# Expert matmuls of a two-layer diffusion step: tokens held in 32-column groups, four quarters of the weights streamed beside each other, 4 KB weight rows, quarter-row scatters, and one activation table set for logarithm and exponential

## The chip, the core and the metric

The kernel runs on one core of one Trainium2 chip. The metric is the device time of one execution in microseconds (us), the median of several runs. All data are 32-bit floats. An fp32 matmul shows in the profile as two records, each with its own weight load.

## The reference

One inference step of a two-layer trunk over 640 tokens of width 1024: 128 context tokens and 512 latent tokens. Each layer is a norm with adaptive modulation, a token mixer (layer 0 an mLSTM, layer 1 a gated DeltaNet, both in two directions), a residual add, a second norm with modulation, and an expert-choice mixture of 16 SwiGLU experts:

```python
aff = softmax((x @ w_router).astype(float32), -1)
gsel, idx = lax.top_k(swapaxes(aff, 1, 2), cap)      # cap = 2 T / 16
xs = x[bidx, idx]
hdn = silu(einsum('becd,edf->becf', xs, w_gate)) * einsum('becd,edf->becf', xs, w_up)
out = einsum('becf,efd->becd', hdn, w_down) * gsel[..., None]
return zeros_like(x).at[bidx, idx].add(out)
```

Each expert takes 64 latent and 16 context tokens (80 in all) and has three weight matrices of 1024 x 1024, 12.58 MB together. The two layers have 32 experts, so 402.7 MB of expert weights are read once each. A final norm closes the trunk.

## The kernel before

The order of work is written out by hand for each engine, with semaphores between them. Per layer: modulation (twelve 2 MB blocks of `w_ada`, two rows of conditioning held in 32 columns, four quarters of the output streamed into PSUM partitions 0, 32, 64, 96: L766), norm and transposes, projections (L809, L810, L819), the scan, `mixer_tail` (`gate_tile`, output projection L1145, second norm, transposes L780, router logits L1151), then `experts`.

`experts` begins on VectorE with softmax and a top-k of ten rounds. TensorE transposes values and indices (L1190, L1191). A gather on GpSimd brings the 80 rows of an expert from `xn_d` into `xs`; `turn` (L1199) transposes them; `tokens` on VectorE (L1742, L1746) applies the modulation and writes `xsT`. `keep_clock` (L1229) is filler work for TensorE before the first expert.

For each expert `hidden` on TensorE (L1210) holds a 128 x 128 block of gate or up weights and streams the 80 tokens past it: 4 slots of 2 MB, 4 column blocks, 8 row blocks, so 128 matmuls or 256 records. ScalarE takes a tanh of the gate part (L689), VectorE makes SwiGLU of it in two operations (L1754, L1757) and writes `hdT`. `down` (L1221) holds 80 columns of `hdT` and streams 512 columns of the down weights: 16 matmuls, 32 records. ScalarE scales the result by the token's gate (L695), and GpSimd scatters 80 rows of 4 KB with accumulation into `moe_d` (L391). The order on TensorE is `hidden(e)`, `turn(e + 1)`, `down(e)`.

The six weight slots are single buffers. Each is loaded again for the next expert once its matmuls are done: slots 1, 3, 5 from the SyncE queue (L336), slots 0, 2, 4 from the ScalarE queue (L683). A slot is half of the columns of a matrix, so a row in HBM is 2 KB. VectorE copies the indices of an expert into `idc` and its gates into `gsc` (L1733, L1734) once the scatter of two experts before has landed.

After the last expert SyncE waits for the last scatter, reads `moe_d` back (L346) and VectorE adds it to `x` (L1784, L1785).

`inverse_root` on ScalarE (L425 Ln, L426 Exp) serves every norm; ScalarE loads a table before each of the two.

Of the kernel before, what the change touches and what calls it, by code (L numbers as in the profile page):

```python
# [24 lines left out]
P = 128  # L25
# [8 lines left out]
CAP = CAPS + CAPP  # L34
HC = 512
# [13 lines left out]
           gathered=256, gexp=32, gmm=1, h_chain=32, hidden=32, idx=16, logits=1, moe_used=96, o_ready=32,  # L49
           omm=10, scattered=256, selt=1, sel=2, sme=1, sm=1, st_new=4, topk=1, x_moe=5, x_new=10, xs_a=64,  # L50
# [3 lines left out]
def backbone(nc, a):  # L54
# [18 lines left out]
    with ctx:  # L73
# [49 lines left out]
        vals = sb("vals", [EX, CAP])  # L123
        idx = sb("idx", [EX, CAP], U32)
        idf = sb("idf", [EX, CAP])
        gsel = sb("gsel", [P, EX])
# [5 lines left out]
        moe_d = nc.dram_tensor("moe_d", [TOK, D], F32, kind="Internal").ap()  # L132
# [3 lines left out]
        osb = [og[:, (2 + q) * D:(3 + q) * D] for q in range(2)]  # L136
        hdT = og[:, 4 * D:4 * D + KT * CAP].rearrange("p (k c) -> p k c", k=KT)
        xsT = [wk[:, q * 640:(q + 1) * 640].rearrange("p (k c) -> p k c", k=KT) for q in range(2)]
        eb = [wk[:, 1280 + q * 320:1600 + q * 320] for q in range(2)]
# [24 lines left out]

        def w_expert(L, e, j):
# [90 lines left out]
        def _(sp):  # L256
# [22 lines left out]
            for L in range(2):  # L279
                for n in range(NADA + NIN):  # L280
                    j = mix_slot(n)
                    if n < 3:
                        if L:
                            sp.wait_ge(S("moe_used"), 6 * (EX - 1) + j + 1)
                    else:
                        sp.wait_ge(*unit_used(L, n - 3))
# [44 lines left out]
                def expert_loads(e, first):  # L331

                    for j in range(6) if first else (1, 3, 5):
                        if not first:
                            sp.wait_ge(S("moe_used"), L * PER["moe_used"] + e * 6 + (j - 5))
                        sp.dma_start(slot[j], w_expert(L, e, j)).then_inc(land[j], 16)  # L336
# [3 lines left out]
                expert_loads(0, True)  # L340
                with sp.Fori(1, EX) as e:
                    expert_loads(e, False)

                sp.wait_ge(S("scattered"), L * PER["scattered"] + 16 * EX)
# [11 lines left out]
        @block.gpsimd  # L356
        def _(pool):
            pool.memset(epst[:, :], EPS).then_inc(S("epst"), 1)

            for L in range(2):  # L360
# [10 lines left out]
                def hold(before):  # L371


                    if not (isinstance(before, int) and before == 0):
                        pool.wait_ge(S("held"), before)
                    pool.tensor_tensor(tick[:, 0:1], epst[0:1, :], epst[0:1, :], ALU.mult).then_inc(S("held"), 1)

                def gather(e, q, first):
                    pool.wait_ge(S("idx"), L * PER["idx"] + e + 1)
                    if not first:  # L380
                        pool.wait_ge(S("xs_turned"), L * PER["xs_turned"] + e - 1)
                    hold(2 * EX * L + e if first else e * 2 + (2 * EX * L - 1))
                    pool.indirect_dma_start(xs[q][0:CAP, :], None, xn_d,
                                            bass.IndirectOffsetOnAxis(ap=idc[q][0:CAP, :], axis=0)).then_inc(S("gathered"), 16)

                def scatter(e, q, first):
                    pool.wait_ge(S("o_ready"), L * PER["o_ready"] + e * 2 + 2)
                    if not first:
                        pool.wait_ge(S("scattered"), L * PER["scattered"] + e * 16)
                    hold(2 * EX * L + (2 * EX - 1) if e is EX - 1 else e * 2 + (2 * EX * L + 2))  # L390
                    pool.indirect_dma_start(moe_d, bass.IndirectOffsetOnAxis(ap=idc[q][0:CAP, :], axis=0),  # L391
                                            osb[q][0:CAP, :], None, compute_op=ALU.add).then_inc(S("scattered"), 16)

                pool.wait_ge(S("xn_out"), 16 * NT * (L + 1))
                pool.wait_ge(S("zero_out"), 16 * NT * (L + 1))
                gather(0, 0, True)
                gather(1, 1, True)
                scatter(0, 0, True)
                gather(2, 0, False)
                scatter(1, 1, False)  # L400
                with pool.Fori(1, EX // 2 - 1) as i:
                    for q in range(2):
                        gather(i * 2 + (q + 1), 1 - q, False)
                        scatter(i * 2 + q, q, False)
                gather(EX - 1, 1, False)
                scatter(EX - 2, 0, False)
                scatter(EX - 1, 1, False)
                pool.wait_ge(S("scattered"), L * PER["scattered"] + 16 * EX)
# [3 lines left out]
        def _(act):  # L412
# [14 lines left out]

            act.wait_ge(S("vec"), 1)
# [224 lines left out]
            def mixer_tail(L):  # L653

                i = 2 * L + 1
                gate_tile(L, 0)
# [18 lines left out]
            def experts(L):  # L675
# [3 lines left out]
                def expert(e, q, first, last=False):  # L679

                    def load(j):
                        if not last:
                            act.dma_start(slot[j], w_expert(L, e + 1, j)).then_inc(land[j], 16)  # L683

                    for hf in range(2):
                        act.wait_ge(S("moe_used"), L * PER["moe_used"] + e * 6 + (2 * hf + 1))
                        if first != 0:
                            act.wait_ge(S("hidden"), L * PER["hidden"] + e * 2 + (hf - 1))
                        A(eb[hf], PS[:, 2 * hf, 0:320], ACT.Tanh, scale=0.5).then_inc(S("gexp"), 1)  # L689
                        load(2 * hf)  # L690
                    for hf in range(2):
                        act.wait_ge(S("moe_used"), L * PER["moe_used"] + e * 6 + (5 + hf))
                        if hf == 0 and first is None:
                            act.wait_ge(S("scattered"), L * PER["scattered"] + (e - 1) * 16)
                        A(osb[q][0:CAP, hf * HC:(hf + 1) * HC], PS[0:CAP, 4 + hf, :], ACT.Copy,  # L695
                          scale=gsc[q][0:CAP, :]).then_inc(S("o_ready"), 1)
                        if hf == 0:
                            load(4)

                expert(0, 0, 0)  # L700
                expert(1, 1, 1)
                with act.Fori(1, EX // 2 - 1) as i:
                    for q in range(2):
                        expert(i * 2 + q, q, None)
                expert(EX - 2, 0, None)
                expert(EX - 1, 1, None, last=True)
# [8 lines left out]
            for L in range(2):  # L715
                norm(2 * L)
# [13 lines left out]
                experts(L)  # L730
            norm(4)
# [3 lines left out]
        def _(pe):  # L735
# [447 lines left out]
            def experts(L):  # L1183
# [6 lines left out]
                tr(PS[0:CAP, 3, 0:EX], vals[:, :], ident[0:EX, 0:EX])  # L1190
                tr(PS[0:CAP, 3, EX:2 * EX], idf[:, :], ident[0:EX, 0:EX]).then_inc(S("selt"), 1)  # L1191
                pe.wait_ge(S("sel"), L * PER["sel"] + 2)

                def turn(e, q, first):
                    pe.wait_ge(S("gathered"), L * PER["gathered"] + e * 16 + 16)
                    if not first:
                        pe.wait_ge(S("xs_in"), L * PER["xs_in"] + e)
                    for kt in range(KT):
                        ins = tr(PS[:, 6 + kt // 4, (kt % 4) * CAP:(kt % 4 + 1) * CAP], xs[q][0:CAP, kt * P:(kt + 1) * P], ident[0:CAP, 0:CAP])  # L1199
                    ins.then_inc(S("xs_turned"), 1)  # L1200

                def hidden(e, q, first):
                    pe.wait_ge(S("xs_in"), L * PER["xs_in"] + e + 1)
                    for j in range(4):
                        pe.wait_ge(land[j], e * 16 + (16 * moe_base(L, j) + 16))
                        if not first:
# [650 lines left out]
```

## Time and profile before

| | us |
|---|---|
| median of 3 runs | 3200.09 (3190.57 to 3201.3) |
| profiled execution, its own time | 3194.56 |
| its span, first to last instruction | 3192.6 |
| TensorE busy | 2937.7 (92%) |
| VectorE, ScalarE, GpSimd busy | 963.5, 567.1, 95.9 |
| DMA | 545.49 MB, mean 171 GB/s |

TensorE's records overlap and their ends are modelled, so a busy TensorE need not be one at its peak. A record of 512 columns is shown as 592 ns at full clock while the next one starts after some 430. The granted clock has two levels, 1.2 and 2.4 GHz; 1.00 in a row is 2.4. The experts of layer 0 run from 741.5 to 1431.1 us of the span, those of layer 1 from 2458.7 to 3148.4.

### The profile page before, as it was taken

The numbers are of one execution on the slowest core, as the hardware profiler recorded it, in microseconds if no ns is written. First come the engines' busy times: TensorE is split into PE (matmuls) and PEld (weight loads), VectorE is DVE, ScalarE is ACT, GpSimd is POOL, SyncE is SP. The second block draws the span as 40 slices with busy tenths as digits, with TensorE's granted clock in tenths as the row PEclk, the third lists the DMA queues.
The fourth block names the chain that finished last, engine by engine and source line by source line (L and its number), as shares of the span: only waits on it lengthen the run. The fifth ranks groups of instructions, "written<-read, shape, count | busy, mean of one in ns | idle before, by whom it ended". The sixth has DMA issues, their size and how long they took to land.

```text
span 3192.6 us, 43116 instructions
## 1 busy us (share of the span) xinstructions
PE 2937.7 (92%) x18357; PEld 2213.0 (69%) x18357; DVE 963.5 (30%) x2409; ACT 567.1 (18%) x1279; POOL 95.9 (3%) x145
## 2 busy tenths in 40 slices
PE   4999999788999999994999989999896999999994
PEld 1565489556778877771665479999845778887773
DVE  1100156542011100002577346677544011100002
ACT  2100111340000000002474112222251000000002
POOL 0000000000000000000000000000000000000000
PEclk8999998888999999997899989999997999999997
DMA  8312000247999999949211000000026899998892
GB/s 355 115 53 73 0 1 1 66 157 255 309 308 305 308 310 305 308 158 385 71 53 53 14 1 1 1 1 1 7 80 239 302 307 307 313 309 303 305 309 82
DMA packets 257932, 545.49 MB, mean 171 GB/s; under 512 B 15233, under 2 KB 23817, under 8 KB 251657
## 3 DMA queue, kind: packets, MB, share of 16 engines
q1 hardware_dynamic: 156617, 328.64, 29.1%
q10 hardware_dynamic: 93600, 188.75, 16.9%
q0 software_dynamic: 7584, 26.22, 3.3%
q8 instruction: 99, 1.62, 0.2%
q14 instruction: 32, 0.26, 0.0%
HBM read 517.89 MB, written 25.70 MB: 170 GB/s over the span
## 4 chain that ended last, share of the span: by engine, by line
PE 85%; DVE 6%; DMA 5%; ACT 3%; issue 1%; SPq 1%; DVEq 0%; POOL 0%; ACTq 0%
PE ps L1210 29%; PE ps L1221 14%; PE ps L809 9%; PE ps L819 6%; PE ps L1145 4%; DMA slots<-in_w_ada_dram 3%; PE ps L1107 3%; PE ps L810 2%; PE ps L1089 2%; PE ps L886 2%; PE ps L1121 1%; PE ps L766 1%; PE ps L797 1%; PE ps L956 1%; PE ps L972 1%; PE ps L968 1%
## 5 line engine op out<-in xcount | busy, mean ns | idle before, releaser
L1210 PEld LDWEIGHTS ps<-wk,slots 128*128 128x128 f32 x6144 | 691.1, 192 | 16.5 <-issue 16.0
L1210 PE MATMUL ps<-wk,slots 128*128 128x80 f32 x6144 | 689.9, 275 | 0.0
L1221 PE MATMUL ps<-qkv,og 128*80 128x512 f32 x1024 | 446.7, 594 | 2.4 <-DVE og L1757 1.3
L1221 PEld LDWEIGHTS ps<-qkv,og 128*80 128x80 f32 x1024 | 151.0, 150 | 275.4 <-issue 268.0
L809 PE MATMUL ps<-hT,slots 128*128 128x512 f32 x640 | 333.3, 603 | 3.3 <-ACT hT L457 3.3
L1210 PE MATMUL ps<-wk,qkv 128*128 128x80 f32 x2048 | 233.9, 275 | 0.0
L810 PEld LDWEIGHTS ps<-hT,slots 128*128 128x128 f32 x640 | 123.2, 193 | 156.1 <-issue 156.1
L1210 PEld LDWEIGHTS ps<-wk,qkv 128*128 128x128 f32 x2048 | 231.3, 192 | 0.0
L819 PE MATMUL ps<-slots,hT 128*128 128x512 f32 x480 | 208.9, 595 | 0.0
L1733 DVE COPY idc<-idT 80x1 uint32 (+1 forms) x32 | 4.8, 149 | 615.1 <-DMA moe_d<-og,idc 615.0
L819 PEld LDWEIGHTS ps<-slots,hT 128*128 128x128 f32 x480 | 91.6, 191 | 111.6 <-issue 111.3
L695 ACT ACTIVATE og<-ps,gsc 80x512 f32<-80x512 f32 x64 | 43.7, 683 | 657.7 <-PE ps L1221 657.7
L689 ACT ACTIVATE wk<-ps 128x320 f32<-128x320 f32 x64 | 28.0, 437 | 717.7 <-PE ps L1210 717.7
L1145 PE MATMUL ps<-slots,qkv 128*128 128x512 f32 x320 | 140.7, 598 | 7.0 <-DMA slots<-in_w_out_dram 4.7
L766 PE MATMUL ps<-slots,cndP 128*32 128x512 f32 x384 | 68.5, 854 | 76.4 <-DMA slots<-in_w_ada_dram 51.9
L1757 DVE SCALAR_TENSOR_TENSOR og<-wk,ps 128x320 f32<-128x320 f32 x64 | 31.2, 487 | 323.9 <-PE ps L1210 323.9
L810 PE MATMUL ps<-hT,slots 128*128 128x128 f32 x640 | 124.1, 276 | 0.0
L1754 DVE SCALAR_TENSOR_TENSOR wk<-wk,ps 128x320 f32<-128x320 f32 x64 | 31.1, 487 | 284.8 <-ACT wk L689 284.1
L1145 PEld LDWEIGHTS ps<-slots,qkv 128*128 128x128 f32 x320 | 60.6, 192 | 80.3 <-issue 75.3
L1495 DVE SCALAR_TENSOR_TENSOR wk<-wk,vecT 128x128 f32<-128x128 f32 x192 | 106.0, 552 | 6.8
L809 PEld LDWEIGHTS ps<-hT,slots 128*128 128x128 f32 x640 | 99.8, 195 | 4.2 <-ACT hT L457 3.7
L1107 PE MATMUL ps<-wk,slots 128*128 128x64 f32 x800 | 100.2, 279 | 2.6 <-DVE wk L1627 2.6
(262 smaller groups left out, 3134.8 us busy)
## 6 DMA issues: line engine op xcount, KB each, us to landing
slots<-in_w_gate_dram ACTq DMA_DIRECT2D x60, 2048.0 KB, 10.1
qkv<-in_w_down_dram SPq DMA_DIRECT2D x34, 2048.0 KB, 9.8
slots<-in_w_up_dram SPq DMA_DIRECT2D x32, 2048.0 KB, 10.1
qkv<-in_w_up_dram SPq DMA_DIRECT2D x32, 2048.0 KB, 7.9
qkv<-in_w_down_dram ACTq DMA_DIRECT2D x30, 2048.0 KB, 7.8
slots<-in_w_ada_dram SPq DMA_DIRECT2D x24, 2048.0 KB, 12.8
slots<-in_w_in_dram SPq DMA_DIRECT2D x16, 2048.0 KB, 8.3
slots<-in_w_out_dram SPq DMA_DIRECT2D x4, 2048.0 KB, 16.4
```

What stands on the lines that cost most here:

```text
L695: A(osb[q][0:CAP, hf * HC:(hf + 1) * HC], PS[0:CAP, 4 + hf, :], ACT.Copy, scale=gsc[q][0:CAP, :]).then_inc(S("o_ready"), 1)
L766: ins = mm(PS[32 * j:32 * (j + 1), g % 2, :], cndP[:, kt, :], aslot[sl][:, kk, j * HC:(j + 1) * HC], start=(kt == 0), stop=(kt == KT - 1))
L809: mm(PS[:, b, :], w, hT[:, kt, P:TOK], start=(kt == 0), stop=(kt == KT - 1))
L810: ins = mm(PS[:, b + 1, 0:P], w, hT[:, kt, 0:P], start=(kt == 0), stop=(kt == KT - 1))
L819: ins = mm(PS[:, 2 * (i % n), :], hT[:, kt, t * P:(t + 1) * P], slot[sl][:, kt, :], start=(kt == 0), stop=(kt == KT - 1))
L886: mm(PS[:, bank, h * P:(h + 1) * P], src[:, h:h + 1].broadcast_to([P, P]), ident, start=(h == 0), stop=False, skip_group_check=True)
L1089: ins = mm(pack(four(PS[:, bx, :])[:, :, 0:64], l)[:, h], B["CM"][l % 2][:, h, :], cols1(B["D"][:, h, :], l, d), start=True, stop=True)
L1107: ins = mm(hb(2 * p + l % 2, h, 64), B["DT"][:, h, :], B["X"][:, h, :], start=True, stop=True)
L1145: ins = mm(PS[:, 6 + j, :], yT[:, kt, t * P:(t + 1) * P], slot[j][:, kt, :], start=(kt == 0), stop=(kt == KT - 1))
L1210: ins = mm(PS[:, j, fb * CAP:(fb + 1) * CAP], slot[j][:, kt, fb * P:(fb + 1) * P], xsT[q][:, kt, :], start=(kt == 0), stop=(kt == KT - 1))
L1221: ins = mm(PS[0:CAP, 4 + j, :], hdT[:, ft, :], slot[4 + j][:, ft, :], start=(ft == 0), stop=(ft == KT - 1))
L1495: ins = V.scalar_tensor_tensor(o_, s, w, o_, ALU.mult, ALU.add)
```

## The change

The 80 tokens are padded to 96 and cut into three groups of 32 (`NGRP`). For gate and up TensorE holds 32 tokens of one row block in each of its four 32-column groups and streams a different quarter of the weight columns past each (256 of gate and 256 of up, 512 in all), so that quarter q lands in partitions 32q to 32q + 31: `gate_up` is 2 halves x 3 groups x 4 row blocks x 4 quarters = 96 matmuls of 512 columns. The hidden values come out with tokens on partitions, so `turn_hidden` transposes them back in six 128 x 128 transposes and ScalarE evacuates them to `hdT`. `down` is 96 matmuls of 256 columns in the same form. The order on TensorE becomes first half of gate and up of e, `turn(e + 1)`, second half, `down(e - 1)`, `turn_hidden(e)`. All loops over experts are unrolled.

A weight block is now half of the rows of a matrix with all columns: 2 MB in rows of 4 KB, all from the SyncE queue. Gathers read their indices from `idT` directly and run up to four experts ahead. The result of an expert is scattered in three DMAs of 128 quarter rows of 1 KB; padded tokens go to 16 extra rows of `moe_d`. Their indices and gates, replicated over the four quarters, come from 24 small matmuls before the first expert.

On ScalarE `log_and_exp` loads the set that holds both functions at five places: the start, each `mixer_tail`, the start of layer 1 and before the final norm.

```diff
+NGRP = 3
+CAPG = 32 * NGRP
+PAD = CAPG - CAP
+HQ = D // 4
...
-        idc = [sb(f"idc{q}", [P, 1], U32) for q in range(2)]
-        gsc = [sb(f"gsc{q}", [P, 1]) for q in range(2)]
+        idQ = sb("idQ", [P, NGRP, EX], U32)
...
+        moe_d = nc.dram_tensor("moe_d", [TOK + PAD, D], F32, kind="Internal").ap()
+        moe_q = moe_d.rearrange("t (q c) -> (t q) c", q=4)
...
         def w_expert(L, e, j):
-            name, hf = (("w_gate", 0), ("w_up", 0), ("w_gate", 1), ("w_up", 1), ("w_down", 0), ("w_down", 1))[j]
-            return a[name][L].rearrange("e (k p) n -> e p k n", p=P)[e, :, :, hf * HC:(hf + 1) * HC]
+            name, hf = (("w_gate", 0), ("w_up", 0), ("w_down", 0), ("w_gate", 1), ("w_up", 1), ("w_down", 1))[j]
+            dst = wdn[hf] if name == "w_down" else wgu[hf][:, j % 3, :, :]
+            return dst, a[name][L].rearrange("e (k p) n -> e p k n", p=P)[e, :, 4 * hf:4 * hf + 4, :]
...
@@ block.sync
+                for e in range(EX):
+                    if e:
+                        sp.wait_ge(S("gu_half"), L * PER["gu_half"] + e)
+                    expert_load(e, 0)
+                    expert_load(e, 1)
+                    if e:
+                        sp.wait_ge(S("gu_done"), L * PER["gu_done"] + NGRP * e)
+                    expert_load(e, 3)
+                    expert_load(e, 4)
+                    if e:
+                        sp.wait_ge(S("dn_half"), L * PER["dn_half"] + e)
+                    expert_load(e, 2)
+                    if e:
+                        sp.wait_ge(S("dn_done"), L * PER["dn_done"] + NGRP * e)
+                    expert_load(e, 5)
...
@@ block.gpsimd
+                def gather(e):
+                    if e >= 2:
                         pool.wait_ge(S("xs_turned"), L * PER["xs_turned"] + e - 1)
+                    hold()
+                    pool.indirect_dma_start(xs[e % 2][0:CAP, :], None, xn_d,
+                                            bass.IndirectOffsetOnAxis(ap=idT[0:CAP, e:e + 1], axis=0)).then_inc(S(f"gathered{e % 2}"), 16)
+                def scatter(e):
+                    if e:
+                        pool.wait_ge(S("scattered"), L * PER["scattered"] + 16 * NGRP * e)
+                    for g in range(NGRP):
+                        pool.wait_ge(S("o_ready"), L * PER["o_ready"] + NGRP * e + g + 1)
+                        hold()
+                        pool.indirect_dma_start(moe_q, bass.IndirectOffsetOnAxis(ap=idQ[:, g, e:e + 1], axis=0),
+                                                osb[e % 2][:, g, :], None, compute_op=ALU.add).then_inc(S("scattered"), 16)
...
+                for e in range(4):
+                    gather(e)
+                for e in range(EX):
+                    if e + 4 < EX:
+                        gather(e + 4)
+                    scatter(e)
...
@@ block.scalar
+            def log_and_exp():
+                nc.scalar.preload_act_table_set("natural_log_exp_and_others")
...
             def mixer_tail(L):
+                log_and_exp()
                 gate_tile(L, 0)
...
+                def gate(e, g):
+                    act.wait_ge(S("gu_done"), L * PER["gu_done"] + NGRP * e + g + 1)
+                    if e:
+                        act.wait_ge(S("hid_tr"), L * PER["hid_tr"] + e)
+                    A(hid[:, g, :], PS[:, g, 0:HQ], ACT.Tanh, scale=0.5).then_inc(S("gexp"), 1)
+                def out(e, g):
+                    act.wait_ge(S("dn_done"), L * PER["dn_done"] + NGRP * e + g + 1)
...
+                    A(osb[e % 2][:, g, :], PS[:, 5 + g, 0:HQ], ACT.Copy, scale=gselT[:, g, e:e + 1]).then_inc(S("o_ready"), 1)
+                def turned_hidden(e):
+                    act.wait_ge(S("hid_tr"), L * PER["hid_tr"] + e + 1)
...
+                    A(hdT[:, 0:2, :, :, :].rearrange("p g b q c -> p (g b q c)"), PS[:, 3, :], ACT.Copy).then_inc(S("hid_ev"), 1)
+                    A(hdT[:, 2, :, :, :].rearrange("p b q c -> p (b q c)"), PS[:, 4, 0:HQ], ACT.Copy).then_inc(S("hid_ev"), 1)
...
@@ block.tensor
+                for k, src in enumerate((idf, vals)):
+                    for g in range(NGRP):
+                        i = 1 + NGRP * k + g
+                        for q in range(4):
+                            ins = mm(PS[32 * q:32 * (q + 1), 3, i * EX:(i + 1) * EX], src[:, 32 * g:32 * (g + 1)], ident[0:EX, 0:EX],
+                                     start=True, stop=True)
...
+                def gate_up(e, hf, g, kt):
+                    for q in range(4):
+                        ins = mm(PS[32 * q:32 * (q + 1), g, :].rearrange("p (a n) -> p a n", a=2), xsT[e % 2][:, 4 * hf + kt, 32 * g:32 * (g + 1)],
+                                 wgu[hf][:, :, kt, q * HQ:(q + 1) * HQ], start=(hf + kt == 0), stop=(hf == 1 and kt == 3))
+                    return ins
+                def down(e, hf, g, kt):
+                    qq, b = divmod(4 * hf + kt, 2)
+                    for q in range(4):
+                        ins = mm(PS[32 * q:32 * (q + 1), 5 + g, 0:HQ], hdT[:, g, b, qq, :],
+                                 wdn[hf][:, kt, q * HQ:(q + 1) * HQ], start=(hf + kt == 0), stop=(hf == 1 and kt == 3))
+                    return ins
...
+                def gate_up_all(e):
+                    pe.wait_ge(S("xs_in"), L * PER["xs_in"] + e + 1)
+                    weights(e, 0, 1)
+                    for kt in range(4):
+                        for g in range(NGRP):
+                            ins = gate_up(e, 0, g, kt)
+                    ins.then_inc(S("gu_half"), 1)
+                    if e + 1 < EX:
+                        turn(e + 1)
+                    weights(e, 3, 4)
+                    for g in range(NGRP):
+                        for kt in range(4):
+                            ins = gate_up(e, 1, g, kt)
+                        ins.then_inc(S("gu_done"), 1)
+                def down_all(e):
+                    pe.wait_ge(S("hid_ev"), L * PER["hid_ev"] + 2 * e + 2)
...
+                def turn_hidden(e):
+                    if e + 1 < EX:
+                        pe.wait_ge(S("xs_in"), L * PER["xs_in"] + e + 2)
+                    for g in range(NGRP):
+                        pe.wait_ge(S("hidden"), L * PER["hidden"] + NGRP * e + g + 1)
+                        for b in range(2):
+                            c = g % 2 * HQ + b * P
+                            ins = tr(PS[:, 3 + g // 2, c:c + P], hid[:, g, b * P:(b + 1) * P], ident)
+                    ins.then_inc(S("hid_tr"), 1)
...
+                for e in range(EX):
+                    gate_up_all(e)
+                    if e:
+                        down_all(e - 1)
+                    turn_hidden(e)
+                down_all(EX - 1)
...
@@ block.vector
+                def hidden(e, g):
...
+                    V.scalar_tensor_tensor(hid[:, g, :], hid[:, g, :], 1.0, PS[:, g, 0:HQ], ALU.add, ALU.mult).then_inc(k, 1)
...
+                    V.scalar_tensor_tensor(hid[:, g, :], hid[:, g, :], 0.5, PS[:, g, HQ:2 * HQ], ALU.mult, ALU.mult).then_inc(S("hidden"), 1)
```

## Rows read from the trace of the kernel before

**Rows 1.** The page's chain that ended last, share of the span by line.

```profile
PE ps L1210 29%; PE ps L1221 14%; PE ps L809 9%; PE ps L819 6%; PE ps L1145 4%; DMA slots<-in_w_ada_dram 3%; PE ps L1107 3%; PE ps L810 2%; PE ps L1089 2%; PE ps L886 2%; PE ps L1121 1%; PE ps L766 1%; PE ps L797 1%; PE ps L956 1%; PE ps L972 1%; PE ps L968 1%
```

**Rows 2.** The chain in order of time: start us, us, what.

```profile
741.54 28.56 PE ps L1210 x256
770.73 13.96 PE ps L1221 x32
...
1417.19 13.97 PE ps L1221 x32
```

**Rows 3.** Windows: stretch, PE, PEld, DVE, ACT, POOL busy, PEclk, DMA share, GB/s.

```profile
13.00:18.00 5.00, 0.89 (x3) 0.46 (x3) 1.26 (x5) 0.21 (x1) 0.00 (x0) 1.00 1.00 410
22.00:32.00 10.00, 4.81 (x28) 1.10 (x32) 2.77 (x10) 9.84 (x16) 0.00 (x0) 1.00 1.01 421
720.00:730.00 10.00, 0.00 (x0) 0.00 (x0) 9.49 (x25) 0.00 (x0) 0.00 (x0) 0.50 1.05 387
800.00:1400.00 600.00, 599.54 (x4117) 472.81 (x4116) 56.65 (x165) 31.39 (x56) 37.30 (x54) 1.00 0.90 306
```

**Rows 4.** Timeline of TensorE: start us, us, engine, line, operation, count [idle before].

```profile
30.83 1.92 PE L766 MATMUL ps<-slots,cndP 128*32 128x512 f32 x16 [1.24 <-DMA slots<-in_w_ada_dram]
31.29 0.13 PEld L766 LDWEIGHTS ps<-slots,cndP 128*32 128x32 f32 x4 [0.30 <-issue]
31.72 0.13 PEld L766 LDWEIGHTS ps<-slots,cndP 128*32 128x32 f32 x4 [0.30 <-issue]
297.40 7.03 PE L819 MATMUL ps<-slots,hT 128*128 128x512 f32 x16
```

**Rows 5.** Groups by form, 800 to 1400 us: busy us, mean ns | idle before.

```profile
L695 ACT ACTIVATE og<-ps,gsc 80x512 f32<-80x512 f32 x28 | 19.1, 684 | 288.1 <-PE ps L1221 288.1
L1754 DVE SCALAR_TENSOR_TENSOR wk<-wk,ps 128x320 f32<-128x320 f32 x28 | 13.7, 488 | 120.0 <-ACT wk L689 119.3 <-issue 0.3
L689 ACT ACTIVATE wk<-ps 128x320 f32<-128x320 f32 x28 | 12.2, 437 | 283.8 <-PE ps L1210 283.8
L1199 PE MATMUL ps<-c,og 80*128 80x80 f32 x112 | 10.1, 232 | 0.0
```

**Rows 6.** DMA, 13 to 18 us: what moved; then the page's software queue.

```profile
DMA packets 537, 2.05 MB, mean 410 GB/s; under 512 B 20, under 2 KB 44, under 8 KB 533
q0 software_dynamic: 7584, 26.22, 3.3%
```

**Rows 7.** Timeline before the first expert of layer 0.

```profile
697.00 10.26 PE L1151 MATMUL ps<-wrt,hT 128*128 128x16 f32 x48
730.93 0.24 PE L1190 MATMUL ps<-c,vals 16*80 16x16 f32 x1 [20.75 <-DVE idf L1723]
731.02 0.22 PE L1191 MATMUL ps<-c,idf 16*80 16x16 f32 x1
```

**Rows 8.** Timeline after the last expert of layer 0.

```profile
1432.30 1.44 POOL L391 DMA_INDIRECT moe_d<-og,idc  x1 [0.16 <-issue]
1437.49 2.55 SPq L346 DMA_DIRECT2D og<-moe_d  x5
```

**Rows 9.** Groups of ScalarE over the whole span: its table loads.

```profile
L425 ACT ACT_TABLE_LOAD x51 | 65.4, 1283 | 0.9
L426 ACT ACT_TABLE_LOAD x51 | 65.4, 1283 | 0.9
```

**Rows 10.** Timeline of the end of layer 0's mixer and of the final norm.

```profile
672.37 13.97 PE L1145 MATMUL ps<-slots,qkv 128*128 128x512 f32 x32 [1.14 <-DVE x L1680]
695.26 1.94 PE L780 MATMUL ps<-c,og 128*128 128x128 f32 x8 [3.70 <-DVE hT L1326]
3176.60 0.15 DVE L1305 TENSOR_SCALAR ss<-ss 128x1 f32<-128x1 f32 x1
3178.57 0.15 DVE L1305 TENSOR_SCALAR ss<-ss 128x1 f32<-128x1 f32 x1
3188.26 1.28 DVE L1317 SCALAR_TENSOR_TENSOR og<-x,ss,wk 128x1024 f32<-128x1024 f32 x1
```

More of the change, by code:

```diff
@@ L330, in _, with expert_load @@
                     sp.dma_start(xn_d[t * P:(t + 1) * P, :], o[:, t, :]).then_inc(S("xn_out"), 16)
[L331 to L336, printed above, removed]
+                def expert_load(e, j):
+                    dst, src = w_expert(L, e, j)
+                    sp.dma_start(dst, src).then_inc(land[j], 16)
                 sp.wait_ge(*unit_used(L, MIX - 1))
                 sp.wait_ge(S("x_new"), L * PER["x_new"] + 10)
[L340 to L344, printed above, removed]
+                for e in range(EX):
[13 more added lines that the diff above has]
+                    expert_load(e, 5)
+                sp.wait_ge(S("scattered"), L * PER["scattered"] + 16 * NGRP * EX)
                 for t in range(NT):
@@ L358, in _ @@
             pool.memset(epst[:, :], EPS).then_inc(S("epst"), 1)
+            held = [0]
             for L in range(2):
@@ L369, in _, with hold @@
                     pool.dma_start(moe_d[t * P:(t + 1) * P, :], zero).then_inc(S("zero_out"), 16)
-                def hold(before):
-                    if not (isinstance(before, int) and before == 0):
-                        pool.wait_ge(S("held"), before)
+                pool.dma_start(moe_d[TOK:TOK + PAD, :], zero[0:PAD, :]).then_inc(S("zero_out"), 16)
+                for q in range(2):
+                    pool.memset(xsT[q][:, :, CAP:CAPG], 0.0).then_inc(S("xs_pad"), 1)
+                def hold():
+                    if held[0]:
+                        pool.wait_ge(S("held"), held[0])
@@ L386, in scatter @@
[L386 to L392, printed above, removed]
@@ L394, in _ @@
-                pool.wait_ge(S("xn_out"), 16 * NT * (L + 1))
[L395 to L404, printed above, removed]
@@ L677, in experts @@
                 A(aff[:, :, :], aff[:, :, :], ACT.Exp).then_inc(S("sme"), 1)
[L679 to L698, printed above, removed]
@@ L708, in modulation @@
+                for e in range(EX + 1):
+                    if e < EX:
+                        for g in range(NGRP):
+                            gate(e, g)
+                    if e:
+                        for g in range(NGRP):
+                            out(e - 1, g)
+                    if e < EX:
+                        turned_hidden(e)
             def modulation(L):
@@ L1189, in experts @@
                 pe.wait_ge(S("topk"), L * PER["topk"] + 1)
[L1190 to L1197, printed above, removed]
+                pe.wait_ge(S("pads"), 5 + PAD)
@@ L1214, in down @@
-                def down(e, q, first):
-                    pe.wait_ge(S("hidden"), L * PER["hidden"] + e * 2 + 2)
-                    for j in range(2):
-                        pe.wait_ge(land[4 + j], e * 16 + (16 * moe_base(L, 4 + j) + 16))
-                        if not first:
-                            pe.wait_ge(S("o_ready"), L * PER["o_ready"] + e * 2 + (j - 1))
-                        for ft in range(KT):
-                            ins = mm(PS[0:CAP, 4 + j, :], hdT[:, ft, :], slot[4 + j][:, ft, :],
-                                     start=(ft == 0), stop=(ft == KT - 1))
-                        ins.then_inc(S("moe_used"), 1)
+                def gate_up(e, hf, g, kt):
[3 more added lines that the diff above has]
+                    return ins
@@ new lines, in down, with weights @@
+                def down(e, hf, g, kt):
[4 more added lines that the diff above has]
+                    return ins
+                def weights(e, *slots):
+                    for j in slots:
+                        pe.wait_ge(land[j], 16 * (moe_base(L, j) + e + 1))
@@ L1727, in experts @@
[L1727 to L1736 removed]
+                V.tensor_copy(idT[0:CAP, :], PS[0:CAP, 3, 0:EX]).then_inc(S("sel"), 1)
@@ L1779, in experts @@
+                tokens(0)
+                for e in range(EX):
+                    if e + 1 < EX:
+                        tokens(e + 1)
+                    for g in range(NGRP):
+                        hidden(e, g)
                 dve.wait_ge(S("g2b"), L * PER["g2b"] + 4)
```

170 lines of the change are left out of this document (72 added, 98 removed).

## The prediction

> **What bounds the kernel now.** The page's chain comes first: TensorE's lines carry it, L1210 with 29% and L1221 with 14%, both of the experts [rows 1]. The chain in order of time then gives the cycle. From 741.54 us on, 256 records of L1210 take 28.56 us and 32 of L1221 take 13.96; the sixteenth expert ends at 1417.19 + 13.97 = 1431.16. That is 689.6 us per layer, 43.1 per expert [rows 2], of which the 8 transposes of `turn` are some 0.6. In the window of 600 us TensorE is busy for 599.54 at full clock while the DMA share is 0.90 at 306 GB/s [rows 3], so nothing else ends last. What the change is worth is read from two rates. Why L1210 is slow is in the quotient: 28.56 / 256 = 0.112 us for a record that streams 80 columns, whereas L1221 needs 13.96 / 32 = 0.436 for 512. Per column that is 1.40 ns against 0.85; L1210's records are paced by their 128-column weight loads and not by the stream.
>
> **TensorE after the change.** The modulation already has the form that the experts get: 32 columns held, four quarters streamed. Its 16 records of 512 columns took 1.92 us at full clock, where 16 ordinary ones took 7.03, and its weight loads come in fours at 31.29 and 31.72, so four records start every 0.43 us [rows 4]. The four quarters do run beside each other, and 1.92 is four such steps plus the tail of the last. Per expert, with two records per matmul:
> - gate and up: 96 matmuls are 192 records, 48 steps of 0.43: 20.6 us (28.56 before);
> - down: 96 matmuls of 256 columns are 48 steps of half the columns, 0.215: 10.3 us (13.96 before);
> - `turn`: 8 transposes, 10.1 us for 112, so 0.7 [rows 5];
> - `turn_hidden`: 6 transposes at L1210's 0.112, so 0.7;
> - four changes between the whole array and its quarters. No row has such a change in a full stream. Below it is nothing; above, I take the tail that an isolated burst shows, 1.92 - 4 x 0.43 = 0.2 each. I take 0.7 together.
>
> The sum is 33.0 us. The down step is the weakest term, since no row streams 256 columns in quarters. Below, its columns bound it at 10.3; above, it could cost as much per step as gate and up do (0.43), 20.6. I take 10.3, because the quarter loads of a step are shown as only 0.13 us for four [rows 4], inside 0.215.
>
> **DMA after the change.** The present stage's weight rows are 2 KB, and with nothing else running they came at 387 GB/s; the start of the kernel, mostly `x` in rows of 4 KB, ran at 410, the 8 KB rows of `w_ada` at 421 [rows 3]. That the first is 4 KB shows in its packets, 2.05 MB in 537 [rows 6]. So 12.58 MB need 12.58 / 0.410 = 30.7 us. The gather adds 0.33 MB; the scatter moves 0.39, and an accumulation also reads what it adds to, so 0.39 to 0.79: 1.8 to 2.7 us at the same rate. Its 384 descriptors of 1 KB instead of 80 of 4 KB may cost more than their bytes; all software DMAs together took 3.3% of the span now, 105 us or at most 3.3 per expert [rows 6], and double the scatter's part would add 1 to 2. DMA needs 32.5 to 33.4, middle 32.9.
>
> TensorE's 33.0 and DMA's 32.9 are level. A load and its use are set apart, though: a block is freed after 10, 21, 27 or 32 us of the cycle and wanted again 10 us or more later than it lands, so neither has to wait for the other's single step and the cycle is the larger of the two. I take 33.2. ScalarE's eight operations per expert are at most 8 x 0.68, and VectorE's six SwiGLU operations at most 6 x 0.49 beside the token operations [rows 5]; both lie beside `down(e - 1)`. SyncE waits for first half, second half, then down's halves, which is TensorE's own order, so no load stands behind a later one. On GpSimd `gather(e + 4)` stands ahead of `scatter(e)` and waits for a transpose in the next expert's first half; `scatter(e)` needs a later point anyway. ScalarE waits for the scatter of three experts before, which has a cycle to land.
>
> **The ends of a layer's experts.** The first expert has no `down` to cover its tanh and SwiGLU of the last group: 0.44 + 0.49 + 0.49 and handovers, 1.7 us [rows 5]. The last `down` waits for the evacuation of `hdT`, under 2 x 0.68, 1.3 us. One `turn` less is -0.7. A layer is 16 x 33.2 + 2.3 = 533.5 against 689.6: 156.1 saved, 312 for both.
>
> The 24 small matmuls before the first gather are 48 records on the path. The two transposes there start 0.09 us apart, at half clock, and a router record with a full weight load takes 10.26 / 48 = 0.21 [rows 7]: 4.3 by the one, 10.3 by the other, and near 1 if the quarters overlap as in the modulation. I take 2.8, less 0.3 for `idc` and `gsc`, which go: +2.5 per layer, +5. After the last expert one scatter took 1437.49 - 1432.30 = 5.2 us, with 1.44 of GpSimd [rows 8]. Three follow each other now at 1.7 us, the groups' pace, and three of GpSimd's may take up to 2 each with 128 rows: 0 to +2, taken as +1 per layer, +2.
>
> **Table set.** 102 table loads of 1.28 us stand before Ln and Exp [rows 9]; 70 of them are in norms and gate tiles and go, the 32 of layer 1's q and k stay. Most are covered: by DMA at the start, by the output projection in the mixer's tail, by modulation in layer 1. On the path are, per layer, TensorE's wait of 3.70 us before the last transpose, of which two loads are 2.6, and 1.14 before the last projection tile, which waits for VectorE behind ScalarE's norms [rows 10]: 7.4 for both. One load stands ahead of layer 1's first gate tile, 1.3. In the final norm ScalarE paces the five tiles; without its loads VectorE does, from 3176.60 in steps of 1.97, ending at 3186.5 where it ended at 3188.26 + 1.28 = 3189.5 [rows 10]: 3.1. Together 11.8. Should the set not be kept, this is nothing.
>
> **Sum.** -312 + 5 + 2 - 12 = -317, against the profiled execution's own 3194.6 (its span is 3192.6): 2878. The median of the runs shown is 5.5 higher, so I say 2880.
>
> **Two rules of the Trainium skill.** TensorE's rows show sixteen quarter records in 1.92 us against 7.03, 3.7 times, and 4.0 times in their steady steps of 0.43 [rows 4]. "TensorE: Matmul & The Clock Gate", section "Measured speedup vs the span model", gives 3.07 times for four row tiles and 2.38 for three column tiles. An estimate from 3.07 would be 20.6 + 10.3 = 30.9 x 4 / 3.07 = 40.3, with 2.1 for the rest 42.4, and a time of some 3170. The steady step speaks against it, the lack of a burst longer than 16 records for it.
>
> The windows of this trace move 410 and 421 GB/s into the core [rows 3]. "DMA: Bandwidth & Descriptors", section "Where 436 GB/s comes from", puts an HBM limit of about 358 per core where its neighbour also streams. Here one core runs, and the trace is above it. By 358 the cycle would be 13.7 / 0.358 = 38 us, some 3030 in all.
>
> **Rivals.**
> - The stream of weights ends last. Where 4 KB rows come no faster than 2 KB rows among the scatters, 13.7 MB at 387 GB/s are 35.4 us [rows 3]; with the dearer small descriptors 36.5. For: the two needs are level, and nobody has shown 4 KB rows beside scatters. Against: 410 and 421. Only fifteen cycles a layer feel it: 15 x 2 x 2.2 to 3.3 = +66 to +99, so 2945 to 2980. Chance 0.18.
> - The quarters do not keep 0.43 and 0.215 in a long stream. If each group of four steps costs 1.92 as in the burst, gate and up are 23.0, down (with the same 0.05 per step) 12.7, the cycle 37.8: +147, 3025. If down's step costs what gate and up's does, 20.6 + 20.6 + 2.1 = 43.3, no gain from the experts, about 3200. Chance 0.11 for a cycle of 35 to 42.5 from this cause, 0.03 for no difference.
> - Slower than before: TensorE's supply of instructions. The cycle has 768 loads and records where it had 576, most for quarter-size work. No long stretch of rows shows them closer than L1210's, 512 in 28.56 us, 0.056 each. At that pace every step of eight costs 0.446, gate and up 21.4, down 21.4, the cycle 44.9: 2 x (16 x 44.9 + 2.3 - 689.6) = +62, less 5 for the rest: 3252. It decides from a down step of about 0.42 on. Against: L1210's pace is explained by its wide loads. Chance 0.05.
> - The change does not do what it says for the tables: the loads stay, +12, 2892. That lies inside the forecast's own spread.
>
> **Chances.** The forecast (cycle 32.3 to 34.5 us, 2850 to 2920) has 0.63. Faster by over 0.5%: 0.63 + 0.18 + 0.11 = 0.92; within 0.5% (16 us, about what a measurement of this kernel can tell from no change) 0.03; slower 0.05. The range 2845 to 2980 takes in the rival of the weight stream and leaves out some 0.19: the slow quarters and what follows them.
>
> **What would show it.** Chain and windows of a layer's middle: a cycle of 33.2 us at full clock. Steps of TensorE: 10.3 us for a half of gate and up, 5.2 for a half of down; a longer down half alone means its small steps, all halves longer alike means the quarters. A wait of TensorE on DMA before gate and up, with the DMA share at 1.00, means the stream; GB/s then tells its rate. Table loads: some 37 at L425 and L426 and the preloads. The experts of a layer outside 515 to 590 us would make the prediction wrong.

## The result, and the profile after

| | us |
|---|---|
| before, median of 4 runs | 3200.12 (3190.57 to 3201.3) |
| after, median of 4 runs | 3518.36 (3514.34 to 3522.01) |
| after / before | 1.1001, 95% interval 1.0977 to 1.1026 |
| predicted | 2880 (2845 to 2980) |

The changed kernel is 10% slower; faster was forecast. The page's chain after, share of the span by line (L1237 is gate and up, L1245 is down), shows what is new against [rows 1]; the line numbers of these two matmuls are others in some of the kernels below:

```profile
PE ps L1237 20%; DMA slots<-in_w_up_dram 17%; PE ps L1245 9%; PE ps L834 8%; PE ps L844 6%; PE ps L1170 4%; DMA slots<-in_w_ada_dram 3%; PE ps L1132 3%; PE ps L835 2%; PE ps L1114 2%; PE ps L911 1%; PE ps L1146 1%; SPq L342 1%; PE ps L791 1%; PE ps L822 1%
```

A transfer carries 17% of the span. The chain in order of time, one cycle of layer 0, answers to [rows 2]:

```profile
819.13 12.69 PE ps L1237 x96
831.82 0.70 PE ps L1231 x8
832.52 10.44 PE ps L1237 x96
842.96 10.40 PE ps L1245 x192
...
853.79 0.59 SPq L342
854.42 20.19 DMA slots<-in_w_up_dram
```

The next cycle's matmuls start at 874.75. TensorE's work is as forecast, but for the first half, which takes 12.69 us here instead of 10.3, and then it stands for 20 us. From the second expert of layer 0 (765.16) to its last (1543.84) are 14 cycles of 55.6 us, where 33.2 were forecast; the 14 of layer 1 are 55.8 each. The windows, in the columns of [rows 3], say the same of the DMA engines:

```profile
800.00:1400.00 600.00, 371.32 (x4200) 148.64 (x4204) 48.28 (x131) 36.20 (x85) 64.05 (x83) 0.80 0.66 242
874.80:908.50 33.70, 33.70 (x393) 13.39 (x394) 4.44 (x12) 2.10 (x5) 3.29 (x6) 0.95 0.41 155
908.50:929.90 21.40, 0.76 (x8) 0.55 (x9) 0.00 (x0) 1.34 (x3) 2.84 (x3) 0.59 1.05 389
```

Over the stage their share is 0.66 and TensorE's clock 0.80. While TensorE works the share is 0.41, inside the wait it is 1.05. So DMA works in full only while TensorE stands, and is idle for more than half of the time in which TensorE works. The reason is in SyncE's timeline, laid beside TensorE's:

```profile
903.32 0.37 SPq L342 DMA_DIRECT2D slots<-in_w_down_dram  x1
908.50 0.37 SPq L342 DMA_DIRECT2D qkv<-in_w_down_dram  x1
908.91 1.61 SPq L342 DMA_DIRECT2D slots<-in_w_gate_dram  x1
910.57 0.67 SPq L342 DMA_DIRECT2D slots<-in_w_up_dram  x1
911.28 4.48 SPq L342 DMA_DIRECT2D qkv<-in_w_gate_dram  x1
```

```profile
903.08 5.36 PE L1245 MATMUL ps<-qkv,wk 128*32 128x256 f32 x96
908.37 0.87 PE L1290 MATMUL ps<-c,wk 128*128 128x128 f32 x6
929.89 11.93 PE L1237 MATMUL ps<-slots,wk 128*32 128x512 f32 x96 [20.64 <-DMA slots<-in_w_up_dram]
```

The loads of gate and up for the next expert go out at 908.91, straight after the down projection ends, although their buffers had been free since the middle and the end of gate and up, some 22 and 11 us earlier.

### The profile page after: what moved, and what is told of

Same layout as the page of the kernel before. It is cut to its first block, busy times and chain, and to the rows that moved or that the text cites. A ratio compares the mean times of both kernels' runs of the same rounds, so it can differ in the third digit from the quotient of the medians.

```text
span 3514.8 us, 49131 instructions
## 1 busy us (share of the span) xinstructions
PE 2684.7 (76%) x21715; PEld 1582.1 (45%) x21715; DVE 976.9 (28%) x2432; ACT 522.4 (15%) x1341; POOL 206.3 (6%) x279
## 4 chain that ended last, share of the span: by engine, by line
PE 69%; DMA 22%; DVE 6%; SPq 1%; ACT 1%; issue 1%; POOL 0%; DVEq 0%; ACTq 0%; POOLq 0%
PE ps L1237 20%; DMA slots<-in_w_up_dram 17%; PE ps L1245 9%; PE ps L834 8%; PE ps L844 6%; PE ps L1170 4%; DMA slots<-in_w_ada_dram 3%; PE ps L1132 3%; PE ps L835 2%; PE ps L1114 2%; PE ps L911 1%; PE ps L1146 1%; SPq L342 1%; PE ps L791 1%; PE ps L822 1%
## 5 line engine op out<-in xcount | busy, mean ns | idle before, releaser
L1237 PE MATMUL ps<-slots,wk 128*32 128x512 f32 x3072 | 398.8, 682 | 587.3 <-DMA slots<-in_w_up_dram 587.3
L1237 PEld LDWEIGHTS ps<-slots,wk 128*32 128x32 f32 x3072 | 114.6, 124 | 851.1 <-issue 851.1
L1237 PE MATMUL ps<-qkv,wk 128*32 128x512 f32 x3072 | 336.2, 593 | 0.0
L705 ACT ACTIVATE wk<-ps 128x256 f32<-128x256 f32 x96 | 36.9, 384 | 1356.9 <-PE ps L1237 1356.9
L1237 PEld LDWEIGHTS ps<-qkv,wk 128*32 128x32 f32 x3072 | 97.0, 110 | 214.2 <-issue 211.6
L1245 PE MATMUL ps<-qkv,wk 128*32 128x256 f32 x3072 | 175.1, 384 | 5.1 <-DMA qkv<-in_w_down_dram 5.1
L1245 PE MATMUL ps<-slots,wk 128*32 128x256 f32 x3072 | 171.7, 379 | 5.1 <-DMA slots<-in_w_down_dram 5.1
L413 POOL DMA_INDIRECT moe_d<-og,idQ x96 | 149.5, 1557 | 30.6 <-POOL tick L397 28.7
L397 POOL TENSOR_TENSOR tick<-epst 1x1 f32<-1x1 f32 x128 | 47.4, 370 | 1580.5 <-PE ps L1231 787.8
L1245 PEld LDWEIGHTS ps<-slots,wk 128*32 128x32 f32 x3072 | 101.1, 110 | 82.5 <-issue 23.5
L1245 PEld LDWEIGHTS ps<-qkv,wk 128*32 128x32 f32 x3072 | 101.2, 111 | 73.4 <-DMA qkv<-in_w_down_dram 6.1
L1815 DVE SCALAR_TENSOR_TENSOR wk<-wk,ps 128x256 f32<-128x256 f32 x96 | 40.5, 422 | 319.7 <-ACT wk L705 319.7
```

Source lines behind the costliest of these rows:

```text
L413: pool.indirect_dma_start(moe_q, bass.IndirectOffsetOnAxis(ap=idQ[:, g, e:e + 1], axis=0), osb[e % 2][:, g, :], None, compute_op=ALU.add). ...
L1237: ins = mm(PS[32 * q:32 * (q + 1), g, :].rearrange("p (a n) -> p a n", a=2), xsT[e % 2][:, 4 * hf + kt, 32 * g:32 * (g + 1)], wgu[hf][:, : ...
L1245: ins = mm(PS[32 * q:32 * (q + 1), 5 + g, 0:HQ], hdT[:, g, b, qq, :], wdn[hf][:, kt, q * HQ:(q + 1) * HQ], start=(hf + kt == 0), stop=(hf ...
```

## The experiments

**The queue's order.** The theory: in the loop over e, SyncE issues gate and up of e, then waits for the down projection of e - 1, which TensorE runs after gate and up of e, and only then comes to gate and up of e + 1. The edit moves the down blocks behind the next expert's gate and up:

```diff
-                for e in range(EX):
...
+                for j in (0, 1, 3, 4, 2, 5):
+                    expert_load(0, j)
+                for e in range(1, EX + 1):
+                    if e < EX:
+                        sp.wait_ge(S("gu_half"), L * PER["gu_half"] + e)
+                        expert_load(e, 0)
+                        expert_load(e, 1)
+                        sp.wait_ge(S("gu_done"), L * PER["gu_done"] + NGRP * e)
+                        expert_load(e, 3)
+                        expert_load(e, 4)
+                    if e >= 2:
+                        sp.wait_ge(S("dn_half"), L * PER["dn_half"] + e - 1)
+                        expert_load(e - 1, 2)
+                        sp.wait_ge(S("dn_done"), L * PER["dn_done"] + NGRP * (e - 1))
+                        expert_load(e - 1, 5)
```

> The changed kernel with SyncE's loads in TensorE's order: blocks 0, 1, 3, 4 of expert e + 1 now stand ahead of blocks 2 and 5 of expert e, which wait for the down projection of e - 1... e's own predecessor. Theory, a queue behind a waiting instruction: in the changed kernel the gate and up loads of the next expert stood behind two waits on a down projection that runs last in the cycle, and TensorE stood 20 us for them. With the order mended the cycle falls from 54.9 to 33.2 us (TensorE 32.7, DMA 32.9) and the time to 2870 to 2900. Rival, the stream itself is slow: the changed kernel's DMA share of 0.66 over a cycle of 54.9 is 36 us of DMA work per expert; then the cycle is 36.3 and the time about 2970, with TensorE waiting some 3 us per expert.

Measured: 2906.87 us (2902.84 to 2913.45), 0.9093 of before (0.9077 to 0.911), the fastest of the kernels here that do the whole work. It is 7 us above the 2870 to 2900 of the theory and far below the rival's 2970. Its windows and TensorE's timeline:

```profile
850.00:1150.00 300.00, 286.33 (x3502) 137.17 (x3498) 37.17 (x100) 30.67 (x71) 53.98 (x70) 1.00 1.04 386
```

```profile
968.18 10.51 PE L1237 MATMUL ps<-slots,wk 128*32 128x512 f32 x96 [1.64 <-DMA slots<-in_w_up_dram]
980.45 10.51 PE L1237 MATMUL ps<-qkv,wk 128*32 128x512 f32 x96 [1.06 <-DMA qkv<-in_w_up_dram]
990.75 5.39 PE L1245 MATMUL ps<-slots,wk 128*32 128x256 f32 x96
995.93 5.39 PE L1245 MATMUL ps<-qkv,wk 128*32 128x256 f32 x96
1002.49 10.51 PE L1237 MATMUL ps<-slots,wk 128*32 128x512 f32 x96 [0.37 <-DMA slots<-in_w_up_dram]
```

The 20 us are gone, the clock is whole, and the DMA share is 1.04. Nine cycles, counted at the start of the second half of gate and up from 910.72 to 1221.97, are 34.6 us each. The order alone is worth 3518 - 2907 = 611 us. The cycle lies between the two expectations, 33.2 and 36.3: TensorE still waits 0.2 to 1.6 us twice per expert.

**Half of the wait.** Gate and up are put between the two down blocks:

```diff
+                    if e >= 2:
+                        sp.wait_ge(S("dn_half"), L * PER["dn_half"] + e - 1)
+                        expert_load(e - 1, 2)
...
+                        expert_load(e, 4)
+                    if e >= 2:
+                        sp.wait_ge(S("dn_done"), L * PER["dn_done"] + NGRP * (e - 1))
+                        expert_load(e - 1, 5)
```

> As the mended order, but gate and up of the next expert stand behind the first block of down (free after half of the down projection) and ahead of the second. Theory of the queue: they are held until half of the down projection is done, and 6.3 MB (one block of down, two of gate and up) then take 15.4 us at 410 GB/s plus 2; TensorE covers 5.9 of it, waits some 11.5, starts cold for 1.7: a cycle of 46, about 3270 us. Rival, the order only moves a wait that the stream makes: no more than the mended order, under 3000.

Measured, one run: 3348.56 us. TensorE's wait:

```profile
965.35 13.27 PE L1238 MATMUL ps<-slots,wk 128*32 128x512 f32 x96 [15.41 <-DMA slots<-in_w_up_dram]
```

The wait shrinks from 20.6 to 15.4 us, by the 5.2 us by which the release is earlier. So the wait follows the place of the load in the queue, with everything else of the change as it was. The cycle is 50.6 us (1015.93 for the next start) where I said 46, and the time 79 us above my 3270, because my number for the wait, 11.5, was too small: from 943.9 to the landing at 965.3 the engines moved 354 GB/s x 21.4 us = 7.6 MB, where I had counted 6.3. The scatters' 0.4 MB and parts of the blocks issued next, some 0.9 MB, were served in the same time.

**Another queue.** The down blocks are loaded from ScalarE's queue, behind the evacuation of e - 1:

```diff
                         for g in range(NGRP):
                             out(e - 1, g)
+                        if e < EX:
+                            for j in (2, 5):
+                                dst, src = w_expert(L, e, j)
+                                act.dma_start(dst, src).then_inc(land[j], 16)
```

> The changed kernel, but the two down blocks of expert e are loaded from the ScalarE queue once the results of e - 1 are evacuated, and SyncE's queue keeps only gate and up. No load order is copied from TensorE's. Theory, head of a queue: what cost the 20 us was that gate and up stood behind waits for the down projection, so taking those waits to another queue does as well as mending the order: a cycle of 34 to 35 us, 2900 to 2920. Rival: it was the mended kernel's finer release (the first down block after half of the down projection) that gave the gain; here both down blocks are released 5 us later, and the cycle would be 38 or more, over 3000.

Measured: 2932.88 us (2926.34 to 2934.08), 0.9178 of before (0.9163 to 0.9193). It loses 26 us to the mended order and lies 13 above the 2920 that I gave it at most, but it is far from the rival's 3000: what matters is that gate and up don't stand behind the down projection, whichever way. Its first down block is issued 5 us later, and between 850 and 1225 us TensorE waits five times, 1.4 to 4.9 us each, for the second half of gate and up. Behind a longer one of these waits that half is slow, at a lower clock:

```profile
882.92 13.32 PE L1235 MATMUL ps<-qkv,wk 128*32 128x512 f32 x96 [3.01 <-DMA qkv<-in_w_up_dram]
```

**TensorE alone.** Weights are loaded for the first expert of each layer only:

```diff
-                        pe.wait_ge(land[j], 16 * (moe_base(L, j) + e + 1))
+                        pe.wait_ge(land[j], 16 * (moe_base(L, j) + 1))
```

> The changed kernel with weights loaded for the first expert of each layer alone; all experts use them, so the expert part of the result is that of other weights. It leaves TensorE's own cycle. Theory: 32.7 to 33.0 us (48 steps of 0.43, 48 of 0.215, 0.7 and 0.7 for transposes, changes between whole array and quarters under 0.2 each), about 2870 us. Rival, long streams of quarters pay for the changes or for instruction supply: a cycle above 34.5.

Measured, one run: 2852.1 us. Window and timeline:

```profile
800.00:1200.00 400.00, 400.00 (x4848) 164.52 (x4844) 53.24 (x144) 41.36 (x96) 73.15 (x95) 1.00 0.15 23
```

```profile
962.38 10.51 PE L1224 MATMUL ps<-slots,wk 128*32 128x512 f32 x96
972.82 0.77 PE L1218 MATMUL ps<-c,og 80*128 80x80 f32 x8
973.52 10.51 PE L1224 MATMUL ps<-qkv,wk 128*32 128x512 f32 x96
983.84 5.36 PE L1232 MATMUL ps<-slots,wk 128*32 128x256 f32 x96
989.02 5.36 PE L1232 MATMUL ps<-qkv,wk 128*32 128x256 f32 x96
994.32 0.88 PE L1277 MATMUL ps<-c,wk 128*128 128x128 f32 x6
995.12 10.51 PE L1224 MATMUL ps<-slots,wk 128*32 128x512 f32 x96
```

The cycle is 995.12 - 962.38 = 32.74 us. A half of gate and up is 24 steps of 0.43 (10.44 and 10.32 to the next start), a half of down 24 of 0.216 (5.18 and 5.30). The half that is followed by whole-array transposes is 0.12 us longer each time, so little is lost between whole array and quarters. Both rivals about TensorE fall here.

**DMA alone, with three loads.** TensorE leaves out two of four row blocks in each half of gate, up and down (`kt in (0, 3)`), which was to leave it some 17 us of work; it was busy for 22 per cycle, at a granted clock of 0.80. The second kernel also has no scatters; the third has the scatters and reads each block in 2 KB rows:

```diff
-            return dst, a[name][L].rearrange("e (k p) n -> e p k n", p=P)[e, :, 4 * hf:4 * hf + 4, :]
+            return (dst.rearrange("p k (h n) -> p (k h) n", h=2),
+                    a[name][L].rearrange("e (k p) n -> e p k n", p=P)[e, :, :, hf * HC:(hf + 1) * HC])
```

> The kernel with the mended order, leaving out half of the row blocks of every expert matmul (two of four in each half), so that TensorE needs some 17 us per expert; all loads, gathers and scatters stay. Theory, the mended kernel is bound by DMA (share 1.04 at 387 GB/s): its cycle stays at 34 to 34.5 us and the time at 2895 to 2915. Rival, its 34.4 come from TensorE's short waits and starts, and DMA alone needs the predicted 32.9: a cycle near 33.

> As the kernel with half of the row blocks, and it also leaves out the scatters. Theory, the scatters' 1 KB rows with accumulation are what the prediction sized too small: weights and gathers alone come at 405 to 410 GB/s, 12.9 MB in 31.7 us, so the scatters cost 2.7 of 34.4. Rival, rows of 4 KB from the expert matrices come no faster than 387 GB/s: 33.3 us, the scatters cost 1.

> As the kernel with half of the row blocks, but each 2 MB block is read in rows of 2 KB (the same bytes and destinations' size, the weights themselves land in other places). Theory, longer rows matter: the cycle rises by the ratio of the shown rates, 410 / 387, to about 36.3. Rival, row length between 2 and 4 KB is nothing: the same cycle as with 4 KB.

Measured, one run each: 2862.41, 2790.96 and 2905.33 us. The same window of the three, in that order:

```profile
850.00:1150.00 300.00, 192.01 (x1800) 75.03 (x1800) 39.94 (x108) 28.74 (x67) 50.20 (x66) 0.80 1.04 389
```

```profile
850.00:1150.00 300.00, 200.20 (x1886) 80.49 (x1890) 39.93 (x108) 30.98 (x72) 9.76 (x18) 0.83 1.03 401
```

```profile
850.00:1150.00 300.00, 178.02 (x1668) 70.13 (x1672) 35.50 (x96) 27.58 (x64) 50.91 (x67) 0.79 1.06 371
```

From landing to landing the cycles are 34.4, 32.4 and 36.2 us (seven, eight and seven of them). With half the matmuls the cycle of the mended kernel, 34.6, hardly moves: it is bound by DMA, as expected. Its time of 2862 is below my 2895 to 2915, because the first and last experts, where the mended kernel goes at TensorE's pace, are shorter with half the matmuls. Scatters cost 2.0 us of the 34.4, and rows of 4 KB instead of 2 KB save 1.8. My price for the scatters, 2.7, and the rival's, 1, both miss; without them the stream runs at 401 GB/s and not at the 410 of [rows 3]. Each of these three is one run of one kernel.

**The cold start after the wait.** In the changed kernel the first half of gate and up takes 11.8 to 13.5 us instead of 10.5, at a clock that fell during the wait. Fillers stand in the wait:

```diff
                     turn_hidden(e)
+                    if e + 1 < EX:
+                        for _ in range(20):
+                            mm(PS[:, 0, :], ident, hT[:, 0, 0:HC], start=True, stop=True)
```

> The changed kernel with 20 filler matmuls (17 us of identity times 512 columns into a free PSUM bank) after each expert's hidden transposes, while TensorE would stand for the loads. Theory: the part of the 20 us wait that the queue makes is untouched, but the first half of gate and up no longer starts at 1.2 GHz: it takes 10.5 instead of 12.0 to 13.5 us, the cycle falls by about 2.2 and the time by 30 x 2.2 = 66, to about 3450. Rival: the time of the cold start is hidden by the loads' pace and comes back as wait: 3518.

> The changed kernel with 23 fillers instead of 20 after each expert's hidden transposes, 19.9 us, so that the gap of 3.8 us before the loads land, in which the clock fell again with 20 fillers, shrinks to about 1. Theory: the first half of gate and up then takes 10.5 instead of 12.0 to 13.4 us, the cycle falls by some 2.2 and the time by 30 x 2.2 to about 3450. Rival: the cold start is hidden, since the loads of the second half and of the next cycle set the pace: 3518, with a wait that grows by what the halves lose.

Measured, one run each: 3520.58 with 20 fillers and 3479.89 with 23, where I had expected about 3450 of both. With 20 a wait of 3.79 us was left, with a granted clock of 0.87 in it and of 0.78 in the half that followed, which still took 13.37. With 23 (the last two lines) the clock was 1.00 in both:

```profile
943.61 13.37 PE L1237 MATMUL ps<-slots,wk 128*32 128x512 f32 x96 [3.79 <-DMA slots<-in_w_up_dram]
...
976.04 19.91 PE L1310 MATMUL ps<-hT,c 128*128 128x512 f32 x46
996.66 10.51 PE L1237 MATMUL ps<-slots,wk 128*32 128x512 f32 x96 [0.71 <-DMA slots<-in_w_up_dram]
```

The half takes 10.51, and the fourteen cycles of layer 0, 783.48 to 1530.01, are 53.3 us, 2.3 less than 55.6. The whole kernel gains 38 and not 66 us: in front of each layer's second expert, where the real wait was only 1.7 and 2.7 us, the fillers add 17 to 18 and take more than half of the gain back. So the first run told only that 17 us of filler are too few; the second puts the cold start at 2.3 us a cycle, by estimate some 65 us of the result (28 x 2.3).

**The table set alone.** The five preloads of the change in the kernel before:

```diff
+            def log_and_exp():
+                nc.scalar.preload_act_table_set("natural_log_exp_and_others")
```

> The kernel before with the one table set alone, loaded at the five places of the change. Theory: 70 of 102 table loads go; on the path they are worth 11.8 us (7.4 in the two mixer tails, 1.3 before layer 1's first gate tile, 3.1 in the final norm): about 3188. Rival: all of it is covered by projection, modulation and DMA: 3200, no difference.

Measured: 3181.41 us, the median of six runs (3172.98 to 3184.78), 0.9945 of before (0.9931 to 0.996), so 13 to 22 us less: small, but clear of no difference. Its table loads, against [rows 9]:

```profile
L425 ACT ACT_TABLE_LOAD x16 | 20.5, 1283 | 0.3
L426 ACT ACT_TABLE_LOAD x16 | 20.5, 1283 | 0.3
L429 ACT ACT_TABLE_LOAD x5 | 6.4, 1283 | 0.8 <-PEq L1853 0.7
```

70 of 102 went, as forecast. TensorE's wait before the last transpose, 3.70 us in [rows 10], where I had counted 2.6 as saved, nearly goes:

```profile
692.79 1.94 PE L788 MATMUL ps<-c,og 128*128 128x128 f32 x8 [0.31 <-DVE hT L1334]
```

The profiled spans differ by 3192.6 - 3181.7 = 10.9, close to my 11.8, but these are two single executions; the medians say somewhat more.

## Why the prediction was wrong, by its steps

**The step that failed** is this one: "SyncE waits for first half, second half, then down's halves, which is TensorE's own order, so no load stands behind a later one." The names of the waits are in TensorE's order, their indices are not. In turn e of the loop `dn_half >= e` asks for the down projection of e - 1, and TensorE runs that after gate and up of e, at the end of the cycle. The next loads of gate and up stand behind it in the same queue. The sentence before it, that a block is freed 10 us or more before it is needed, was true of the buffers and said nothing of the queue. The size can be estimated: after the down projection the second down block, two blocks of gate and up and the scatters have to come, 6.3 + 0.4 MB, which at the 387 GB/s of [rows 3] is 17 us. The profile shows 20 us, because the engines served 389 GB/s x 21.4 us = 8.3 MB in the wait: 1.6 MB of the other blocks in flight came with them. The wait of 20.6 and the slow first half of 2.3 on TensorE's 32.7 give 55.6. 28 such cycles times 22.4 us (55.6 - 33.2) are 627 of the 638 us that I missed, and mending the order gave 611 back. The mended kernel's 2907 lies inside the forecast range of 2845 to 2980, so the sum was near for a kernel in this order, but not for the one that was to be judged.

**The step was not among the rivals.** All of them priced rates: of the stream, of the quarters, of instructions. The one for slower was about TensorE's instruction supply, and the run without loads refutes it: 768 loads and records in 31.2 us, 0.041 each, and in a half of down 192 in 5.18, 0.027 each, closer than L1210's 0.056.

**Steps that held**, against the kernel without loads: gate and up 20.8 (20.6 said), down 10.5 (10.3), `turn` 0.7, `turn_hidden` 0.8 (0.7), the cycle 32.74 (33.0). The changes of array shape, for which I had taken 0.7, are no more than 0.24 and are inside the first two. The weakest term, down's step, came out at its lower bound, which the weight loads of [rows 4] had spoken for. The steady step of 0.43 of a 16-record burst was the right reading. The 3.07 times that the Trainium skill's "TensorE: Matmul & The Clock Gate", section "Measured speedup vs the span model", gives for four row tiles would by estimate have made gate and up 26.9 us and would have missed: in this stream the quarters run 4 times as fast as one after another.

**DMA's need** was put at 32.9 us and is 34.4. Of the 1.5 missing, 0.7 is the stream (401 GB/s for 410: 12.9 MB in 32.2). The scatters took 2.0, where the sum had 1.0 to 1.9 for their bytes and nothing for their small rows; in the profile they count 0.39 MB per expert, not 0.79. What is left, some 0.2, is not explained. That makes the mended kernel 2907 and not 2880; this rival ("the stream of weights ends last", 2945 to 2980) named the right bound with too high a price.

**The small terms.** The 24 small matmuls overlap in their quarters and take some 0.8 us in all, for 2.8:

```profile
728.37 0.52 PE L1221 MATMUL ps<-c,idf 16*32 16x16 f32 x24
728.71 0.50 PE L1221 MATMUL ps<-c,vals 16*32 16x16 f32 x24
```

After the last down matmul, which ends at 1594.2, `moe_d` is read 5.0 us later (1599.2) where it was 6.3 before [rows 2, 8]: the three scatters add nothing, I had said 1. The final norm went as forecast: its last operation ends at 3511.7, 22.5 us after the first addition, for 25.5 before.

## What to carry to other kernels

A single queue that waits is a program of its own: write its waits down with their indices beside the cycle of the engine that releases them, and ask of each what is queued behind it; a freed buffer starts no load. A mean DMA share of 0.66, with 1.05 inside the waits and 0.41 outside them, meant here that transfer and work took turns, and that the order, not the rate, was to be mended. When two bounds come out level, as here, look at the handover between them as well: that is where nearly the whole miss was.

## What the runs showed of the hardware

- Four quarters of the array, each with 32 columns held, sustain four fp32 streams: 0.43 us per step of 512 columns over 96 records and 0.216 per step of 256 over 192, with 0.12 us lost at a change to whole-array transposes (the kernel without loads, one run).
- TensorE's granted clock was 0.87 in a wait of 3.8 us and 0.78 in the half after it, which took 13.4 us (20 fillers); with a wait of 0.7 us it was 1.00 in both and the half took 10.5 (23 fillers).
- In the same stage with half of the matmuls left out, 2 KB rows came at 371 GB/s in all and 4 KB rows at 389 (one run each); 384 accumulating quarter rows per expert cost 2.0 us of DMA time for 0.39 MB (cycles of 34.4 and 32.4 us with and without them).
